# Attention stage of a hybrid mixer kernel: VectorE takes the second map's maximum and the gate ahead of the hyena's spectra products

## What is computed

```python
def _diff_scores(q, k, v, lam):
    s = jnp.einsum('bqhmd,bkhmd->bhmqk', q, k).astype(F32) * DIFF_SCALE
    p = jax.nn.softmax(s, axis=-1)
    attn = p[:, :, 0] - lam * p[:, :, 1]
    return jnp.einsum('bhqk,bkhe->bqhe', attn.astype(v.dtype), v)

def _fft_long_conv(u, kf, bias):
    uf = jnp.fft.rfft(u.astype(F32), n=2 * L, axis=1)
    y = jnp.fft.irfft(uf * kf, n=2 * L, axis=1)[:, :L]
    return (y + bias.astype(F32) * u.astype(F32)).astype(u.dtype)
...
z = x1 * _fft_long_conv(v, kf[:, 0], bias[0])
return x2 * _fft_long_conv(z, kf[:, 1], bias[1])
```

## Time and profile before

| quantity | value |
|---|---|
| time, median of 3 runs | 3986.91 us (3985.05 to 3989.5) |
| profiled execution: time, span | 3983.79 us, 3982.0 us |
| mean granted TensorE clock | 0.944 |
| busy share of the span, PE / DVE / ACT / POOL | 87% / 63% / 27% / 25% |
| attention stage of layer 0, layer 1 (about) | 1103 to 1562 us, 3075 to 3537 us |

### The profile page before, as it was taken

The page is one execution under the profiler, slowest core; times in us unless marked ns, Lnnn a source line. Parts: engine busy times, 40 slices in busy tenths (PEclk is TensorE's granted clock), DMA queues, the critical chain, the costliest instruction groups (busy, mean ns, idle before and its releaser), DMA issues. The chain is left out here.

```text
span 3982.0 us, 50563 instructions
## 1 busy us (share of the span) xinstructions
PE 3466.1 (87%) x19076; PEld 2835.3 (71%) x19076; DVE 2494.0 (63%) x4816; ACT 1089.6 (27%) x1979; POOL 999.7 (25%) x702
## 2 busy tenths in 40 slices
PE   6999999999668876996897889999998688859898
PEld 2788888888557775675784577888887577747577
DVE  4135467675469996775564324657775599967665
ACT  2112122211244444331310211222211455523221
POOL 4233333332001111210221423433442011122121
PEclk8999999999789998998898999999999799979999
DMA  5354232232163321433525255223322633133442
GB/s 208 67 161 136 78 100 85 89 96 71 54 191 94 78 61 52 135 99 118 165 85 195 73 120 167 93 82 100 95 91 62 191 88 88 39 106 108 118 139 76
DMA packets 414869, 423.46 MB, mean 106 GB/s; under 512 B 57008, under 2 KB 351408, under 8 KB 413474
## 3 DMA queue, kind: packets, MB, share of 16 engines
q1 hardware_dynamic: 368644, 315.22, 27.6%
q10 hardware_dynamic: 45984, 105.01, 7.6%
HBM read 287.76 MB, written 124.01 MB: 103 GB/s over the span
## 5 line engine op out<-in xcount | busy, mean ns | idle before, releaser
L751 PE MATMUL l_p_acc<-l_u_hi,l_w_hi 128*128 128x512 f32 (+1 forms) x2208 | 605.7, 376 | 21.2 <-PEq L158 9.0
L751 PE MATMUL l_p_acc<-l_u_hi,l_w_lo 128*128 128x512 f32 (+1 forms) x2208 | 588.0, 368 | 0.0
L751 PE MATMUL l_p_acc<-l_u_lo,l_w_hi 128*128 128x512 f32 (+1 forms) x2208 | 587.1, 367 | 0.0
L751 PEld LDWEIGHTS l_p_acc<-l_u_hi,l_w_hi 128*128 128x128 f32 x2208 | 384.1, 189 | 98.6 <-issue 26.0
L751 PEld LDWEIGHTS l_p_acc<-l_u_hi,l_w_lo 128*128 128x128 f32 x2208 | 381.2, 189 | 72.0
L751 PEld LDWEIGHTS l_p_acc<-l_u_lo,l_w_hi 128*128 128x128 f32 x2208 | 381.2, 189 | 71.8
L664 POOL TENSOR_TENSOR l_w_hi<-l_wt,l_p_zero 128x1024 fp32r<-128x1024 f32 x100 | 203.2, 2032 | 905.0 <-PE l_p_acc L751 750.2
L1517 PE MATMUL l_at_pS<-l_at_k_hi,l_at_q 128*128 128x512 f32 (+1 forms) x400 | 166.8, 417 | 145.0 <-ACT l_at_prob L1632 85.2
L666 POOL TENSOR_TENSOR l_w_lo<-l_wt,l_w_hi 128x1024 fp32r<-128x1024 f32 x100 | 264.3, 2643 | 7.8
L2446 PE MATMUL l_o_pA<-l_o_w_hi,l_o_o_hi 128*128 128x512 f32 x576 | 225.4, 410 | 42.5 <-DVE l_o_o_lo L2552 35.5
L1735 DVE TENSOR_REDUCE l_at_nmax<-l_at_pS 128x1 f32<-128x1280 f32 (+1 forms) x144 | 197.1, 1369 | 99.1 <-PE l_at_pS L1518 93.8
(11 more groups left out here) (328 smaller groups left out, 7174.5 us busy)
## 6 DMA issues: line engine op xcount, KB each, us to landing
l_wt<-w_in SPq DMA_DIRECT2D x104, 512.0 KB, 3.9
l_n_wa<-w_ada SPq DMA_DIRECT2D x10, 2048.0 KB, 16.6
kf_d<-l_p_R SPq DMA_DIRECT2D x72, 256.0 KB, 3.6
l_o_oT<-o_d SPq DMA_DIRECT2D x18, 1024.0 KB, 6.8
xbc_d<-l_p_fin ACTq DMA_DIRECT2D x28, 640.0 KB, 2.9
l_at_K<-kf_d SPq DMA_DIRECT2D x64, 256.0 KB, 2.9
l_o_rows<-w_out SPq DMA_DIRECT2D x32, 512.0 KB, 4.6
qk_d<-l_p_late ACTq DMA_DIRECT2D x12, 1280.0 KB, 4.6
```

Of the source, the lines that this page charges most:

```text
L751: mm = pe.matmul(acc[:, a:a + w], (w_hi, w_lo)[wp][m % 2][:, k], (u_hi, u_lo)[up][:, k, t0 + c:t0 + c + w], start=(k == n == 0), stop=(k = ...
```

## The change

On VectorE, `products(n)` moves from between `combine(i - 1)` and `maximum(i, 1)` to behind `gate(i - 4)`, ahead of the butterflies. No instruction is added or removed, no wait is changed, and the streams of the other engines stay as they are.

```diff
                         maximum(i, 0)
                     if 1 <= i < NU + 1:
                         combine(i - 1)
-                    if step_of(i) is not None:
-                        products(step_of(i))
                     if i < NU:
                         maximum(i, 1)
                     if 4 <= i < NU + 4:
                         gate(i - 4)
+                    if step_of(i) is not None:
+                        products(step_of(i))
                     p, part = divmod(i - FIRST_STEP, 4)
```

## The result

The kernel after takes 4042.32 us (median of 4 runs, 4035.18 to 4050.01) against 3986.59 before (4 runs, 3985.05 to 3989.5). The ratio is 1.0144, with a 95% interval of [1.0122, 1.0166]: 55.7 us slower. The forecast was 4035, with a range of 4010 to 4068. The profiled execution after took 4035.18 us, with a span of 4033.4.

A forecast was written before the change was run, and what follows sets the result against it. VectorE's own work sets the pace; the new order makes it wait. Layer 1 29.3 + layer 0 27.9 - 9.4 given back = 47.8 us: 4031.6 profiled, 4035 as a median; own range 4018 to 4055, whole range 4010 to 4068.

The forecast's parts named there:

- part 2, full, from 17 on: Full part 2 iterations: no wait at map 1's maximum, as `combine` runs until 5.39 us; slower TensorE clock costs 0.7 each.
- context units: Layer 0, six iterations with short scores needing no exponential first: between nothing and 0.38 us, 0.2 each, 1.3 together.
- given back at 9 and 13: Both layers: earlier gate lets `turn_rows` split TensorE's idle time; 12.9 us instead of 15.24, -2.35 four times, -9.4.
- The second maximum: Map 1's maximum on VectorE waits for its last piece of scores: 1.62, 0.38, none, 1.28 us in parts 0 to 3.
- The ring: Closed chain: map 1's maximum, gate, products, `backward`, `forward`, turn, copy, exponential, map 1's maximum; 8.42 + 3.72 = 12.14 us.
- The floor of 3.75 us: Map 1's maximum starts at earliest 3.75 us after map 0's (last piece 3.21, plus 0.54), so VectorE waits 0.38.
- The gain of 0.43 us: Part 2: products run after GpSimd's `differences` instead of beside it; between nothing and 0.43 us saved, taken as 0.43.
- my upper bound of +0.72: Part 2: largest change expected per iteration, if TensorE's clock falls; lower bound -0.43 if it stays up; 0.7 taken.
- the price is 1.22: Part 2: after about 3.1 us idle, TensorE's `backward` at 1.2 GHz takes 3.08 us instead of 1.86; 0.07 slack comes off.
- Faster: Rival, chance 0.07: only gains at iterations 9 and 13 and in part 2, -13 us, 3974; mean wait under 0.1 us.
- no change: Rival, chance 0.05: mean waits between 0.1 and 0.45 us, paid by what is given back; 3979 to 3995 us.
- The clock falls all over: Rival, chance 0.12: TensorE's idle times hold 1.2 GHz for `backward` in most of 50 iterations, 4095 us; half, 4065.

The follow-up runs named there:

- cut map: Kernel after, map 1 of full latent units made over 1024 keys, without its last piece: 3992.43 us, ratio 1.0018; same cut in the kernel before: 3975.85 us.
- the filled old order: Kernel before plus 16 unused matmuls behind `values` in part 2 of each phase from iteration 9 on: 3989.64 us, ratio 1.0012.
- the gate-first version: Kernel before with only the gate moved ahead of the products in iterations 9 and 13 of either layer: 3979.57 us, ratio 0.9979.
- half with parts 1 and 3: Kernel after with the products back at their old place in parts 0 and 2, so the new order in parts 1 and 3 alone: 4009.35 us, ratio 1.0065.

## Why the prediction was right, and where its sizes were off

| group of iterations, both layers | forecast us | measured us |
|---|---|---|
| part 0, full | 19.2 | 17.9 |
| part 1, full | 4.0 | 4.6 |
| part 2, full, from 17 on | 4.9 | 7.1 |
| part 3, full | 14.3 | 13.7 |
| iterations 3 to 5 | 6.8 | 6.2 |
| context units (10, 11, 20, 21, 30, 31) | 1.3 | 4.5 |
| first full map behind one (12, 22, 32) | 4.2 | 6.0 |
| end of the stages | 2.5 | 2.1 |
| given back at 9 and 13 | -9.4 | -6.2 |
| sum | 47.8 | 55.7 |

The entries are rounded, the sum is that of the exact ones. The direction, the path and most terms were right. The sum of the forecast is 7.9 us short, for the most part in three terms: the context units with those behind them (5.0), what is given back (3.2) and part 2 (2.2).

**The second maximum.** Forecast at 4.99, 3.75, 5.39 and 4.65 us in parts 0 to 3, measured at 4.99, 3.73, 5.39 and 4.65. The waits shown (1.54, 0.28, none, 1.20) are some 0.1 shorter than forecast, because a row's end lies behind the next row's start. The lengths of 13.5, 12.55 and 12.35 came out at 13.54, 12.53 and 12.37. Part 0 is 1.3 us below the forecast because I counted iteration 31 of layer 1, which has no next maximum to be measured to. The cut map showed that all these waits come from the last piece. The stages grew by 30.3 and 25.4 us, for 20 to 28 expected.

**The ring.** Forecast 12.14 us; iterations 4 and 5 took 12.14 to 12.26 in both layers.

**The floor of 3.75 us** was too high: undisturbed, the second maximum starts at 3.54 to 3.55 us. "The earliest that this piece came is 3.21 us" was a wrong reading already of the trace of before. In iteration 2, from which the earlier trace rows are, the first maximum starts at 1125.25, so the piece came 3.00 us behind it (1128.25) and the second maximum 3.54 (1128.79).

```profile
1125.25 1.49 DVE L1735 TENSOR_REDUCE l_at_nmax<-l_at_pS 128x1 f32<-128x1280 f32 x1 [4.11 <-PE l_at_pS L1518]
```

That part 1 came out all the same is luck, two errors that cancel. The products of part 0 are six instructions instead of four, so in the kernel after from its second maximum to `backward` are 3.86 us and not 3.72; that leaves 8.54 - 3.86 = 4.68 us to the next iteration, whose map 1 is ready at 8.42 - 4.68 = 3.74. Measured are 3.73. The ring held part 1, where I had the floor. The run with the gate behind the products agrees: `backward` came 0.2 us sooner and part 1 fell to 3.54.

**Part 2.** The gain of 0.43 us from products that no longer run beside GpSimd is exact where the clock stayed up: 12.92 against 13.35 us, with L1777 at 0.42 us instead of 0.67. The clock's price was too small. I took 14.0 us; of seven instances from iteration 17 on one took 12.92 and six 14.29 to 15.64, and five of these six lie over my upper bound of +0.72 by 0.2 to 0.4 us, one by 1.6. The term that was mis-sized is "the price is 1.22". It counts only the 16 loads of `backward`, but the turn and the scores behind them are slow too. From `backward` to the next maximum TensorE took 5.41 us at a mean granted clock of 0.68 in iteration 25 of layer 0, and 3.81 us at 1.00 in iteration 13 of layer 1:

```profile
1419.67:1425.08 5.41, 5.41 (x29) 5.21 (x30) 3.74 (x15) 1.80 (x6) 0.00 (x0) 0.68 0.22 61
3301.86:3305.67 3.81, 3.80 (x29) 3.63 (x30) 3.74 (x15) 1.68 (x6) 0.00 (x0) 1.00 0.35 104
```

In iteration 25 of layer 1 `backward` was only 0.31 us longer, but four loads of the turn took 0.87 us instead of 0.47, and VectorE waited 1.59 us. Over the six instances the wait was 1.40 to 2.75 us.

```profile
3459.96 2.17 PEld L1590 LDWEIGHTS l_at_pH<-l_at_R,l_at_inv 128*128 128x128 f32 x16 [3.25 <-DVE l_at_R L1777]
3462.01 0.87 PEld L1533 LDWEIGHTS l_at_pT<-ident,l_at_mix 128*128 128x128 f32 x4
```

**Given back.** -2.58, -0.43, -0.74 and -2.45 us for a forecast of -2.35 each. The mechanism is right, as two of the four show, and the run with the gate alone ahead shows it in all four. The timeline after, iteration 9 of layer 0, has the idle time split into 1.27 and 1.55 us as forecast:

```profile
1215.82 0.42 PEld L1560 LDWEIGHTS l_at_pT<-ident,l_at_hx 128*128 128x128 f32 x4 [1.27 <-issue]
...
1217.79 1.86 PEld L1590 LDWEIGHTS l_at_pH<-l_at_R,l_at_inv 128*128 128x128 f32 x16 [1.55 <-DVE l_at_R L1777]
```

In iteration 13 of layer 0 and 9 of layer 1 the clock fell with it, and waits of 2.89 and 1.62 us followed. The failed step is "the iteration should be 12.9 us", taken for all four.

**Context units.** The step "short scores that need no exponential first: between nothing and the 0.38 of the floor" failed for part 0. Iterations 11 and 31 cost 1.78 and 1.77 us: the short second maximum waits 1.4 us, and the gate 1.06 more, with the products behind it. Iterations 10 and 30 cost 0.42 and 0.56, with the gate waiting 0.45; 20 and 21 cost nothing. Of those behind them 22 cost 3.2 us where I had 1.4.

**Rivals.** "Faster" and "no change" needed a mean wait below 0.45 us at the second maximum; it was about 1. "The clock falls all over" held in most of part 2 and at 12, 22, 23 and 32 of layer 0, and not in the rest: in part 3 `backward` kept its 1.86 us behind 1.40 us of idle time. The forecast's own range of 4018 to 4055 holds the time.

**What stays open.** What makes the clock fall in one instance and not in the next. The same question stands behind iterations 22 and 37 of layer 0, which took 1.0 and 1.6 us more than before in the kernel with the gate first at 9 and 13 and in both with the rows behind `backward`. There the loads of `backward` took 1.86 us in iteration 21 and 3.53 in 22, where they had been 2.99 and 1.87: the fall came one iteration later, where it costs. Iteration 37 took 1.5 to 1.6 us more in two other kernels too (the filled old order, the gate first in every part 2). In it, with the gate first at 9 and 13, the 20 loads of `values` took 4.39 us instead of 2.31. And how large the gain of the gate-first version is: its interval excludes no change, but it lies near the 0.2% that can be told at all, and with the gate ahead in every part 2 the interval reaches 1.0002.

## What to carry to other kernels

Before a consumer is moved to "its data are long ready", follow what the producer itself waits for: here a shared bank made map 1's last piece depend on map 0's maximum, exponential and turn, so it was better that VectorE did its 2 us of independent products between the two maxima. Ask also whom each of the two steps feeds: the products feed TensorE, whose next scores wait behind `backward`, the second maximum only ScalarE, whose exponential is not joined before the next iteration. When a change costs time but gives some back in a few places, look for the one instruction that gives it: the gate alone in two iterations gave 0.2%, at the edge of what can be told here.

## What the runs showed of the hardware that was not expected

The same idle time of TensorE ahead of the same 16 loads had two outcomes within one execution: behind 3.24 us they took 2.98 or 1.86 us (kernel after), behind 2.1 us 2.61 or 1.86 (half with parts 1 and 3), and 3.24 or 1.86 already in the kernel before (iterations 29 of layer 1 and of layer 0, 2.09 us each); behind 4.75 us they took 3.49 (cut map). A turn of rows in the middle of the gap did not always help: in the kernel after a last piece of 1.55 us went before loads of 1.86 us (iteration 9 of layer 0) and of 2.73 (iteration 9 of layer 1). The Trainium skill, TensorE: Matmul & The Clock Gate, "HAM oscillation", warns of idle gaps between bursts of matmuls; the long ones here bear it out, and the gap next to the burst does not decide alone.

In the kernel before VectorE's two products with both inputs in SBUF take 0.60 to 0.67 us beside GpSimd (1.78 and 2.56 in one instance each) and 0.42 without it, while those that read PSUM keep their 0.68. By the Trainium skill, GPSIMD Engine Reference, Key points, GpSimd contends with VectorE instructions that have two SBUF inputs, and the traces agree.
